# A one-core encoder layer: the stick-breaking stage written as one pipeline over its head pairs

## What is computed

```python
def sb_attend(q, k, v, q_pos0):
    z = jnp.einsum('bqhd,bkhd->bhqk', q, k).astype(jnp.float32) * SCALE
    vis = jnp.arange(nk)[None, :] < (q_pos0 + jnp.arange(nq))[:, None]
    log_fail = jnp.where(vis, jax.nn.log_sigmoid(-z), 0.0)
    log_w = z + lax.cumsum(log_fail, axis=3, reverse=True)
    w = jnp.exp(jnp.where(vis, log_w, NEG))
    out = jnp.einsum('bhqk,bkhd->bqhd', w.astype(v.dtype), v)

def merge(oa, ob, ga, gb, w_br_a, w_br_b, w_out):
    return (jax.nn.sigmoid(ga) * (oa @ w_br_a) + jax.nn.sigmoid(gb) * (ob @ w_br_b)) @ w_out
```

## Time and profile before

| | us |
|---|---|
| median of 3 runs | 1681.58 (1680.41 to 1681.86) |
| the profiled execution, its span | 1681.6 |
| stick-breaking stage, first product to last matmul | 268.7 to 678.4 |
| of it, one iteration of the loop | 102.4 |
| gap on PE before the merge | 678.4 to 684.3 |
| PE busy over the span | 1590.9 (95%) |

### The profile page before, as it was taken

One profiled execution on the slowest core, in us unless ns is written; L12 is line 12 of the kernel. 1 busy time (PEld: TensorE's weight loads), 2 busy tenths in 40 slices (PEclk: granted clock), 3 DMA queues, 4 the chain that ended last, 5 costly groups with the idle time before them and its releaser, 6 DMA issues.

```text
span 1681.6 us, 27158 instructions
## 1 busy us (share of the span) xinstructions
PE 1590.9 (95%) x9750; PEld 1456.5 (87%) x9750; DVE 767.6 (46%) x1319; ACT 558.3 (33%) x1167; POOL 476.3 (28%) x404
## 2 busy tenths in 40 slices
PE   6998999989898898898999999999999999999996
PEld 5987998878797887897888898998989989899894
DVE  6363473765847668745543313223132231322318
ACT  6354364444443344533333121211212112121123
POOL 2101111342423424242004232322323223232234
PEclk9999999999999999999999999999999999999998
DMA  6111212121021211345222111201112012021123
GB/s 182 49 52 47 61 43 61 44 70 51 25 72 42 57 51 50 122 146 184 105 79 67 50 54 34 62 25 50 57 30 62 27 48 62 26 62 32 43 101 143
DMA packets 129922, 110.44 MB, mean 66 GB/s; under 512 B 14472, under 2 KB 118192, under 8 KB 129872
## 3 DMA queue, kind: packets, MB, share of 16 engines
q1 hardware_dynamic: 122960, 101.11, 19.6%
q10 hardware_dynamic: 6912, 8.65, 1.4%
HBM read 87.94 MB, written 21.80 MB: 65 GB/s over the span
## 4 chain that ended last, share of the span: by engine, by line
PE 77%; issue 9%; DVE 8%; ACT 3%; POOL 1%; DMA 1%; SPq 0%; ACTq 0%; POOLq 0%; DVEq 0%
PE m_ya L1493 20%; PE m_yb L1493 10%; PE m_yb L1515 9%; PE b_gm L893 8%; PE a_gm L443 6%; PE a_gm L479 4%; PE m_ya L1515 4%; DVE b_fail L1073 3%; PE b_gm L915 3%; PE m_ya L1546 3%; PE m_yb L1546 2%; PE b_tb L990 2%; DVE b_wgt L1076 1%; PE a_ob L544 1%; ACT b_wgt L873 1%
## 5 line engine op out<-in xcount | busy, mean ns | idle before, releaser
L1312 POOL TENSOR_TENSOR w_lo<-f_raw,w_hi 128x1024 fp32r<-128x1024 f32 x66 | 157.9, 2399 | 406.5 <-ACT w_hi L1363 406.5
L1493 PE MATMUL m_ya<-x_hi,w_hi 128*128 128x352 f32 x704 | 227.3, 323 | 1.2 <-DVE x_lo L1628 0.9
L1493 PE MATMUL m_ya<-x_lo,w_hi 128*128 128x352 f32 x704 | 225.6, 320 | 0.0
L1493 PE MATMUL m_ya<-x_hi,w_lo 128*128 128x352 f32 x704 | 225.6, 320 | 0.0
L1363 ACT ACTIVATE w_hi<-f_raw 128x1024 fp32r<-128x1024 f32 x66 | 68.2, 1050 | 213.3 <-PE m_yb L1483 209.3
L1493 PEld LDWEIGHTS m_ya<-x_hi,w_hi 128*128 128x128 f32 x704 | 132.0, 188 | 2.5 <-issue 1.0
L1493 PEld LDWEIGHTS m_ya<-x_hi,w_lo 128*128 128x128 f32 x704 | 132.3, 188 | 0.4
L1493 PEld LDWEIGHTS m_ya<-x_lo,w_hi 128*128 128x128 f32 x704 | 132.0, 187 | 0.0
L1681 DVE TENSOR_TENSOR f_yacc<-m_yb,f_yacc 128x512 f32<-128x512 f32 x132 | 90.9, 690 | 82.0 <-PE m_yb L1515 81.6
L1493 PE MATMUL m_yb<-x_hi,w_hi 128*128 128x352 f32 x352 | 113.6, 323 | 0.0
L1493 PE MATMUL m_yb<-x_hi,w_lo 128*128 128x352 f32 x352 | 113.0, 321 | 0.0
(11 more groups left out here) (245 smaller groups left out, 3961.2 us busy)
## 6 DMA issues: line engine op xcount, KB each, us to landing
f_raw<-in_w_gate_up_dram SPq DMA_DIRECT2D x44, 512.0 KB, 3.9
w_raw<-in_w_in_dram SPq DMA_DIRECT2D x33, 512.0 KB, 4.0
f_raw<-in_w_down_dram SPq DMA_DIRECT2D x22, 512.0 KB, 3.4
m_gate<-gate_scratch SPq DMA_DIRECT2D x16, 528.0 KB, 4.3
gate_scratch<-a_gst ACTq DMA_DIRECT2D x24, 176.0 KB, 1.9
gate_scratch<-b_gst ACTq DMA_DIRECT2D x24, 176.0 KB, 1.9
xtok<-in_x_prompt_dram SPq DMA_DIRECT2D x8, 512.0 KB, 3.4
w_raw<-in_w_out_dram SPq DMA_DIRECT2D x8, 512.0 KB, 4.1
```

The lines of the kernel that those rows point to most:

```text
L1312: pool.tensor_tensor(w_lo[:, j % 3, :, :].rearrange("p k n -> p (k n)"), raw[:, j % 2, :], w_hi[:, j % 3, :, :].rearrange("p k n -> p (k n ...
L1493: last = pe.matmul(gm[c][:, 0:CW], w[:, j % 3, k, :], x[:, k, chunk(c)], start=(k == 0 and n == 0), stop=(k == KT - 1 and n == 2))
```

## The change

The loop over pairs becomes straight code of 36 steps s (`NS`; pair s // 9, i = s % 9). In front of it stand only the products of the first pair. The products of the next pair (q, k, v) and the gates take the place of the fill: `products(first, count)` runs through all 20 tiles in one order, `STEP` says how many matmuls a step gets (288 over the nine steps of a pair, 348 in the last pair, and `LAST` 12 behind), `fills` cuts that number into the same four kinds of pieces. q, k and the turned v have two buffers each; v has a bank `b_vvt` of its own beside `b_kvt`. ACT now makes the plain copies of k and v, and reads finished chunks out between the scores of the two heads of a step (`chunks(s, False)`) and after the output copy (`chunks(s, True)`). The cached keys are turned in step 5, the k and v of the next pair in steps 6 and 7. The last piece of fill of a step stands behind the products with v, not ahead of them.

The head outputs go to a DRAM scratch `o_scratch`, branch A's by ACT's queue, branch B's in three parts a pair by SP, and come back in three chunks of 1.4 MB into buffers that overlay those of the first pairs. Chunks 0 and 1 are split by ACT and DVE at the end of steps 34 and 35 (4 + 4 instructions of 704 columns each), chunk 2 in the merge stage. The first weight tile of the merge is split in the stage too. The number of matmuls, turns, scans and masks is unchanged.

```diff
-                with pe.Fori(0, NIT) as p:
...
-                    for c in range(NCH):
-                        pe.wait_ge(gate_out, past(p * GATES - (c < 2)))
-                        gemm(p, 0, c)
...
+            STEP = [[6, 19, 26, 33, 40, 46, 54, 60, 4]] * (NP - 1) + [[8, 24, 33, 42, 50, 58, 66, 55, 12]]
+            LAST = 12
...
+            def fills(s):
...
+                if s == NS:
+                    return 0, 0, 0, LAST
+                f, i = STEP[s // NT][s % NT], s % NT
+                z, g = f // 8, f // 10 if s and GROUPS[(s - 1) % NT] > 1 else 0
+                rest = f - z * PIECES[i] - 2 * g
+                return z, rest // 2, g, rest - rest // 2
...
+                products(0, 8 * MM)
+                tokens("k", 0)
+                products(8 * MM, MM)
...
+                for s in range(NS + 1):
...
+                    nz, na, ng, nc_ = fills(s)
...
+                    products(at, na)
+                    at += na
+                    if s < NS and i == 5:
+                        pe.wait_ge(cache_loaded, 80 * (pair + 1))
+                        for a in range(2):
+                            t = TURN["c", pair, a]
+                            need(pe, turned_out, t - 1)
+                            for b in range(CB):
+                                last = pe.transpose(tb[t % 2][:, b * P:(b + 1) * P], kc[:, a, b, :], ident[:, :])
...
+                    if i in (6, 7) and pair < NP - 1:
+                        tokens("kv"[i - 6], pair + 1)
...
+                        last.then_inc(o_done, 1)
+                    products(at, nc_)
+                    at += nc_
```

ACT, in the middle of a step, and DVE at its end:

```diff
+                            if a:
+                                for r in chunks(s, False):
+                                    chunk_out(r)
+                                if i == 5:
+                                    for b in range(2):
+                                        act.wait_ge(turned, TURN["c", pair, b] + 1)
+                                        act.activation(kch[:, b, :], tb[TURN["c", pair, b] % 2][:, 0:PAST], ACT.Copy).then_inc(kc_hi, 1)
...
+                    if s in (NS - 2, NS - 1):
+                        for e in range(4):
+                            split_o_lo(dve, s - (NS - 2), e)
...
-                for c in range(NCH):
-                    for k in range(KT):
-                        dve.wait_ge(o_hi_ready, c * KT + k + 1)
-                        dve.tensor_tensor(o_lo[:, k, chunk(c)], ot[:, k, chunk(c)], o_hi[:, k, chunk(c)].bitcast(F32),
-                                          ALU.subtract).then_inc(o_lo_ready, 1)
+                for e in range(4):
+                    split_o_lo(dve, 2, e)
```

More of the change, by code:

```diff
@@ L103, in bank, with need @@
         return ctx.enter_context(nc.psum_tensor(name, [P, 512], F32))
+    def need(engine, semaphore, count):
+        if count > 0:
+            engine.wait_ge(semaphore, count)
     with ExitStack() as outer:
@@ L108, in build @@
         epst = sb(outer, "epst", [P, 1])
+        passed = sem("passed")
         x_hi = sb(outer, "x_hi", [P, KT, TOKENS], F32R)
@@ new lines, in build, with filled @@
+            LAST = 12
[6 more added lines that the diff above has]
+                return z, rest // 2, g, rest - rest // 2
+            def filled(s, end):
+                before = sum(sum(fills(e)[1:]) + fills(e)[2] + fills(e)[0] * PIECES[e % NT] for e in range(s))
+                z, a, g, c = fills(s)
+                return before + (z * PIECES[s % NT] if s < NS else 0) + a + (2 * g + c if end else 0)
@@ new lines, in chunks @@
+            def chunks(s, end):
+                upto = 3 * NCH + filled(s, end) // MM
+                since = 3 * NCH + (filled(s, False) if end else filled(s - 1, True) if s else 0) // MM
+                return range(since, upto)
+            ORDER = [("k", 0, n) for n in range(3)]
+            for s in range(NS + 1):
+                pair, i = divmod(s, NT)
+                if s < NS and i == 5:
+                    ORDER += [("c", pair, a) for a in range(2)]
+                if s == 0:
+                    ORDER += [("v", 0, n) for n in range(3)]
+                else:
+                    ORDER += [("w", s - 1, g, a) for g in range(GROUPS[(s - 1) % NT]) for a in range(2)]
+                if i in (6, 7) and pair < NP - 1:
+                    ORDER += [("kv"[i - 6], pair + 1, n) for n in range(3)]
@@ L731, in blocks_of, with piece @@
+            TURN = {key: n for n, key in enumerate(ORDER)}
+            def piece(s, a, j):
+                pair, i = divmod(s, NT)
+                return pair * NZ + 2 * sum(PIECES[:i]) + a * PIECES[i] + j
             def blocks_of(i):
@@ new lines, in _ @@
+                lo(2)
+                los(range(3 * NCH))
+                for s in range(NS):
+                    q = ROWS[s % NT]
+                    for a in range(2):
+                        hs = 2 * s + a
+                        pool.wait_ge(z_read, piece(s, a, PIECES[s % NT] - 1) + 1)
+                        for buf, slot, fill in ((fail, hs % NF, 1.0), (wgt, hs % NW, 0.0)):
+                            diag = buf[0:q, slot, SEQ - q:SEQ]
+                            pool.affine_select(out=diag, in_=diag, compare_op=ALU.is_gt, fill=fill, base=0,
+                                               pattern=[[-1, q]], channel_multiplier=1).then_inc(masked, 1)
+                    if s:
+                        los([*chunks(s - 1, False), *chunks(s - 1, True)])
@@ new lines, in chunk_out, with out @@
+                    if c == 1 and 3 <= T + 2 < NTILE:
+                        hi(T + 2)
+                    if c == 0 and T == NTILE - 1:
+                        act.wait_ge(m_raw_loaded[0], 32)
+                        act.activation(w_hi[:, 0, :, :], m_raw[0], ACT.Copy).then_inc(m_first_hi, 1)
+                def out(s):
+                    pair, i = divmod(s, NT)
+                    act.wait_ge(o_done, s + 1)
+                    need(act, o_stored[i // 3], 16 * pair)
+                    act.activation(ot[:, toks(i)], ob[:, 0:ROWS[i]], ACT.Copy).then_inc(o_out, 1)
```

695 lines of the change are left out of this document (367 added, 328 removed).

## The result

The changed kernel takes **1709.94 us** (median of 4 runs, 1708.96 to 1710.24) against 1681.72 us beside it: ratio 1.0165, 95% interval 1.0151 to 1.0179. It is 28 us slower; 15.9 were forecast. The profiled execution has a span of 1708.2 us, 26.6 more than the one before.

A forecast was written before the change was run, and what follows sets the result against it. PE was taken to set the pace, busy 93.4 of 102.4 us an iteration. Three middle pairs +13.5, last pair +1.4 and boundary +1.0 on 1681.6 gave 1697.5 us, range 1670 to 1720.

The forecast's parts named there:

- (1): Products with v, steps 1 to 4 and sample rows: no fill hides DVE's copy any more, +2.5 us a pair.
- (2): Cached keys turned in step 5: the next turns wait for ACT's copy and DVE's subtraction, +1.8 us a middle pair.
- (3): Second head's scores: PE waits for ACT to read the bank, mainly in steps 5 and 6, +2.0 us a pair.
- (4): Turns of weights: waits vanish in steps 1 to 7, 3.2 us left in step 8, -0.7 us a pair.
- (5): Step 8: no product between its four turns, each waits for a copy of 0.69 us, +0.4 us a pair.
- clock behind long waits: Slow PE clock after waits inside the steps: no cost forecast; a slow clock there would break the boundary's term.
- (6): Register instructions: constants replace wait counts in registers, saving idle time at PE's weight loads, -1.5 us a pair.
- Boundary and last pair: Handover to the merge +1.0 us (10.4 against 9.4); last pair, without k chunk and tokens, +1.4 us.
- Rival C: Shared port: two more of four weight splits a pair reach PE's path, 2.2 us each, 1715 us; chance 0.17.
- Rival A: Pipeline fills as meant: twice the fill hides (2) to (4), period under 88 us, 1658.6 us; chance 0.22.

The follow-up runs named there:

- the kernel with filled waits: Changed kernel with unread 128-column matmuls in PE's long waits, their counts cut to end within each wait: 1709.16 us, ratio 1.0162.
- the five edits: The four edits plus a STEP row of sizes 6, 19, 30, 41, 40, 42, 50, 48, 12 for the first three pairs: 1672.73 us, ratio 0.9938.
- The four edits: Changed kernel with fill before products with v, cached keys first, weights' low parts on DVE, chunk 0 and 1 subtractions behind the last copies: 1674.72 us, ratio 0.9945.
- the sizes: Changed kernel with another STEP row for the first three pairs, no k chunk ending with step 4; alone 1711.86 us, ratio 1.0175.

## Why the prediction was right in sign and short in size

Direction and range held. The size was 12 us short. Per pair, from start to start on PE's timeline, less what the matmul in front of the wait takes by itself (a wait in brackets leaves out some 0.2 us of that matmul's way through, so these are larger than the brackets), and against the shares of 89.3, 90.9 and 90.9 us:

| term | forecast | measured |
|---|---|---|
| (1) products with v bare | +2.5 | +3.7 |
| (2) cached keys | +1.8 | +2.4 |
| (3) second head's scores | +2.0 | +1.6 |
| (4), (5) turns of weights | -0.3 | -2.5 |
| clock behind long waits | 0 | +1.5, +1.4, +1.5 |
| (6) register instructions, and the rest | -1.5 | +1.8, +1.7, +1.8 |
| sum | +4.5 | +8.5, +8.3, +8.5 |

The last row is what is left over, not a measurement of its own. Over three pairs the forecast is 11.8 us short: 9.8 by the last row, 4.4 by the clock, 3.6 and 1.8 by (1) and (2), and 7.8 the other way by (3) to (5). That it came as near as it did is in part luck.

- **(1) was mis-sized, and its reasoning was only half right.** The forecast priced each hand-over by the products that hid it, 0.48 or 0.64 us. But the latency grew as well where the two heads' turns stood apart before, by a wait for the multiply: one copy was then made already, and now both follow the last turn. DVE in step 3, before and after:

```profile
522.51 0.56 DVE L1061 COPY b_wt<-b_tb 128x384 f32<-128x384 f32 x1 [0.17 <-PE b_tb L990]
...
424.51 1.02 DVE L1186 COPY b_wt<-b_tb 128x384 f32<-128x384 f32 x2 [2.68 <-PE b_tb L1101]
```

And the step from cover lost to time lost was not valid by itself: in the kernel before the same move costs nothing. It does cost in the changed kernel, where PE has no other wait in steps 1 to 4 that could get shorter.

- **(2)** was near its upper bound of 2.5, and its undoing took the wait away.
- **(3)** had the right places and sizes (forecast 2.3 in step 5, measured 2.14). In step 6 the forecast blamed the three k chunks on DVE; the scan beside POOL's split is 1.4 of the 2.25 us.
- **(4)** Right that steps 1 to 7 wait no more and one wait of about 3 us is left (3.2 forecast, 2.81 measured). The saving was larger: the old waits, start to start, took 6.7 us and not 5.3, those of the changed kernel 4.0.
- **(6) failed.** The rest of a pair did not get cheaper by 1.5 us but dearer by 1.8. Of this, 1.3 us is step 8: under the slow stretch 32 products with v take 3.28 us (401.18) where they take 1.97 (398.89) in the kernel with filled waits, and PE would else wait there for the sample rows' weights, for which the forecast had no term. That leaves +0.5 where -1.5 was forecast. That idle time of the weight loads with no releaser was a cost of PE was never shown. Whether cuts between kinds of matmuls ate it wasn't tried, so the cause stays open.
- **Clock.** The prediction looked for a slow clock only at the merge and put it at nothing in the steps. It comes behind waits of 2 us inside the steps too, in the kernel before as well. In the changed kernel every pair has a stretch behind the wait of step 5 that costs 1.5 us (8.19 us to the turns in all three pairs, 6.65 where the clock stays up), and the second and third have one more, which is why they are 1.4 and 1.6 us longer than the first with the same waits. Before, only the second and third had one.
- **Boundary and last pair**: forecast +2.4, measured 26.6 - 25.3 (three pairs) - 1.1 (the stage starts at 269.86 instead of 268.74) = +0.2. The boundary's waits were as forecast (3.02 and 3.42 for 3.6 and 3.9; 1.90 for 2; 1.16 for 1), but 13.7 us at the lower level came with them, against 6.8 before. So the last pair must have been cheaper than forecast; how wasn't broken down. Behind the first matmul of the merge (711.63 instead of 684.33) 0.7 us are won back.
- **Rival C** (the port, 1715 us) was given 0.17 and is part of what happened: slowed scans on PE's path cost some 2.1 us a pair, where the rival had 4.4 and the forecast 0.9. Their undoing gave 10.4 us, part of it by the clock.
- **Rival A** fails with periods of 97.8 to 99.4 where it needed 88. With the five edits the periods are 87.6, 89.2 and 89.6 us (from 334.36, 422.00, 511.20 and 600.83), 1.3 to 1.7 below the shares of the kernel before, where A had 4.5. The four edits and the sizes bring a part of A, and the fill alone brought none of it.

## What to carry to other kernels

Don't price a lost cover by the latency that it hid: ask which wait comes next behind the moved work, for that one gets shorter by as much; only where none follows is it paid nearly in full. When waits are merged into fewer and longer ones, look at the granted clock behind each, not only at the sum of the waits. And an engine's side work (here a weight split on POOL, a chunk readout on ACT) is cheap by its total and dear by its place: four such placements, each a few lines, were worth 8 to 17 us apiece (with the slow stretches of the clock that went with some of them), while a table of sizes only moved the waits about.
